# Two expert layers in one kernel: the last experts of a layer taken singly, the closing norm by halves, the first experts found in eights, and ring places freed one at a time

## The chip, the cores and the metric

One core of one Trainium2 chip runs the whole program. The metric is the device time of one execution in microseconds (us).

## The reference

The input is 256 tokens of width 1024, worked on as two tiles of 128 tokens. A first block (pooling, dilated attention, gates) is followed by a second block of two layers. Each of these layers has a mixer (a short convolution in layer 0, windowed attention in layer 1) and then an expert part, which is what the change is about. Cut to it:

```python
def _peer(xn, w_q, subkeys, u_tab, v_tab):            # 8 heads, 128 keys, 16 experts a head
    q = (t @ w_q).reshape(n_tok, PEER_HEADS, 2, SUB_DIM)
    sc = jnp.einsum("thpd,hpnd->thpn", q, subkeys)
    sv, si = lax.top_k(sc, PEER_TOPK)
    cand = sv[:, :, 0, :, None] + sv[:, :, 1, None, :]      # 16 x 16 candidates
    top_v, pos = lax.top_k(cand, PEER_TOPK)
    idx = jnp.take_along_axis(cidx, pos, axis=-1)
    g = jax.nn.softmax(top_v, axis=-1)
    ...
    h = jnp.einsum("cd,ced->ce", xc, jnp.take(u_tab, ic, axis=0))
    a = gc * jax.nn.gelu(h, approximate=False)
    return jnp.einsum("ce,ced->cd", a, jnp.take(v_tab, ic, axis=0))

for i in range(DEPTH_2):                              # 2 layers
    x = x + mixer_i(_rmsnorm_2(x, ...))
    x = x + _peer(_rmsnorm_2(x, ffn_norm_g[i]), ...)
return _rmsnorm_2(x, final_norm_g)
```

Each token picks 128 experts in each layer, each of them a row of 2048 f32 numbers (1024 for the dot, 1024 for the output).

## The kernel before

**Units, pairs and the ring.** In a layer, a unit is one head of one tile: 16 units (`UNITS`), the first eight for tile 0, the others for tile 1. One gather fetches, for each of the 128 tokens, the row of its e-th expert of the unit: 128 x 2048 f32, 1 MB. `ring` has eight places (`RING`) for such gathers. All steps go by pairs of experts (`GROUP` is 2), eight pairs to a unit and 128 pairs to a layer; n counts them.

**The path of a pair.** GpSimd (POOL) issues two gathers (line 534) once `ring_free` says that the pair that had the places is used up. VectorE (DVE) computes a dot for each expert as it lands (`dots`, line 1508) and raises `dots_done` after the second. ScalarE (ACT) then does `mix`: Gelu of both dots (line 666), the product with the gate for each (line 671), and a diagonal matrix 128 x 128 for each, the identity scaled by that coefficient (line 676). TensorE (PE) multiplies each diagonal with the second half of its expert's row, in two halves of 512 columns, into the tile's accumulator in PSUM (`weighted`, line 1117), and raises `ring_free` after the pair. psA is the accumulator of tile 0, psB that of tile 1.

**Around the pairs.** Between the dots, DVE finds the experts of the next unit (`topk_keys`, `topk_grid`, `topk_pairs`, `topk_onehots`, `topk_experts`; the last raises `expert_ready`, for which the gathers of that unit wait) and its gates. For the first unit of a layer all of these steps run ahead of the first dot. In layer 1 they stand ahead of the attention of tile 1 (`attend(1)`). Query products and other matrix products are spread over the slots n of PE's loop by hand-written tables (`PART_SLOTS`, `Q2_AT`).

**The end of a layer.** After the last pair, `tile_out(1)` adds psB to x (line 1516), ACT squares the row and sums it (`norm`, line 548), DVE makes the reciprocal root from a guessed start and three Newton steps in a chain of small instructions, each waiting for the one before (lines 1256 to 1263), and scales the row (line 1265, or 1268 with gains). In layer 1 this is the final norm, and SP then stores the tile (line 485). In layer 0 it is the norm of the attention: PE turns the tile (`turn(3, 1, xn)`), ACT and DVE copy it out (`turned_out`), and PE computes keys (`tile_keys`), scores and values of tile 1 for `attend(0)`. The row's `queries2_out(0, 1, psC)` on DVE copies out the last queries of tile 0. The bias tables of the attention, `bias2[0]` (POOL's queue, line 540) and `bias2[1]` (SP's), and the output weights `wo2` lie where the ring is, so they are loaded only when `ring_free` says that the layer's last pair is used up.

```python
            # PE between the layers
            for j in (2, 3):
                tile_queries(psC[:, 512:1024], 0, 1, j)
            pe.wait_ge(xn_done, step(4, 1))
            turn(3, 1, xn)
            turned_in(3, 1)
            pe.wait_ge(v2_copied, 1)
            tile_keys(1, 0)
            tile_keys(1, 1)
```

## Time and profile before

| | |
|---|---|
| median of three runs | 1900.3 us (1897.44 to 1901.44) |
| the profiled execution | 1901.83 us, with a span of 1899.9 us |
| mean granted TensorE clock | 0.974 of full |
| PE busy | 1645.2 us, 87% |
| DVE, ACT, POOL busy | 55%, 29%, 32% |
| moved by DMA | 642.53 MB, mean 338 GB/s |
| gathers (queue q0) | 540.92 MB, 69.3% of the 16 engines' span |

The profile is of one execution. Its instructions lie within the span; the execution's own time is 1.9 us longer. A clock of 1.00 is the upper level of TensorE's two (2.4 GHz), 0.50 the lower (1.2 GHz); a stretch with a number between holds some of both.

### The profile page before, as it was taken

What the parts mean: (1) busy time and instruction counts of PE and PEld (TensorE: products, weight loads), DVE (VectorE), ACT (ScalarE), POOL (GpSimd) and SP (SyncE); (2) the same over time, 40 slices, a digit from 0 to 9 for tenths busy, and PEclk for the clock granted to TensorE, in tenths of its full rate; (3) what the DMA queues carried; (4) which work ended last, traced back from release to release, by engine and by line L of the source; (5) the groups of instructions that cost most, each with busy time, mean ns of one, the idle gap of its engine ahead of it and who ended that gap; (6) DMA issues with size and microseconds to landing.
All of it is one profiled execution on the core that took longest, in us unless ns stands there. A gap on an engine that the chain in (4) does not pass through costs nothing.

```text
span 1899.9 us, 18599 instructions
## 1 busy us (share of the span) xinstructions
PE 1645.2 (87%) x6184; PEld 958.7 (50%) x6184; DVE 1048.3 (55%) x2676; ACT 554.5 (29%) x1665; POOL 598.6 (32%) x532
## 2 busy tenths in 40 slices
PE   7999999998779988887987779898998988877776
PEld 6888886985335444443542336653544443333222
DVE  2211202224776666576776643666676667676664
ACT  1211000101333433333334323332333333333332
POOL 1000000002444433345444420143444443454442
PEclk9999999999999999999999999999999998899999
DMA  9444333565999999999999987799999999999996
GB/s 227 128 130 159 113 133 130 182 251 211 421 404 398 421 417 417 417 413 390 421 420 413 421 327 248 299 356 413 420 421 421 411 421 399 412 418 416 421 422 266
DMA packets 152926, 642.53 MB, mean 338 GB/s; under 512 B 9972, under 2 KB 50052, under 8 KB 87037
## 3 DMA queue, kind: packets, MB, share of 16 engines
q0 software_dynamic: 74976, 540.92, 69.3%
q1 hardware_dynamic: 77852, 100.42, 15.9%
q8 instruction: 49, 0.80, 0.2%
q14 instruction: 49, 0.39, 0.1%
HBM read 640.19 MB, written 1.11 MB: 338 GB/s over the span
## 4 chain that ended last, share of the span: by engine, by line
PE 33%; DMA 31%; issue 20%; DVE 9%; ACT 4%; POOL 3%; DVEq 0%; POOLq 0%; ACTq 0%
DMA arena<-in_peer_uv,arena 31%; PE ps L1117 17%; DVE arena L1508 5%; PE ps L813 4%; POOL arena L534 3%; PE ps L824 2%; PE ps L995 2%; ACT arena L676 1%; PE ps L1051 1%; ACT arena L671 1%; PE ps L793 1%; ACT arena L666 1%; PE ps L1041 1%; PE ps L1025 1%; PE ps L1082 0%
## 5 line engine op out<-in xcount | busy, mean ns | idle before, releaser
L1117 PE MATMUL ps<-arena 128*128 128x512 f32 x2048 | 979.1, 624 | 217.5 <-ACT arena L676 217.3
L534 POOL DMA_INDIRECT arena<-in_peer_uv,arena x512 | 587.3, 1147 | 1076.9 <-PE ps L1117 580.3
L1508 DVE CUSTOM_DVE_ANT_0 arena<-xn,arena 128x1024 f32<-128x1024 f32 x512 | 622.2, 1225 | 372.3 <-DMA arena<-in_peer_uv,arena 361.1
L1117 PEld LDWEIGHTS ps<-arena 128*128 128x128 f32 x2048 | 385.9, 197 | 755.7 <-issue 401.8
L666 ACT ACTIVATE arena<-arena 128x2 f32<-128x2 f32 x256 | 52.1, 204 | 822.3 <-DVE arena L1508 821.9
L676 ACT ACTIVATE arena<-const,arena 128x128 f32<-128x128 f32 x512 | 177.5, 394 | 8.3
L793 PE MATMUL ps<-hT,wbuf 128*128 128x256 f32 x704 | 153.0, 379 | 1.1 <-DMA wbuf<-in_w_in 1.1
L793 PEld LDWEIGHTS ps<-hT,wbuf 128*128 128x128 f32 x704 | 133.4, 190 | 19.7 <-issue 1.5
L671 ACT ACTIVATE arena<-arena 128x1 f32<-128x1 f32 x512 | 123.2, 288 | 8.4
L995 PEld LDWEIGHTS ps<-hT,wbuf 128*128 128x128 f32 x736 | 88.2, 192 | 18.7 <-issue 17.7
L995 PE MATMUL ps<-hT,wbuf 128*128 128x128 f32 x736 | 88.7, 275 | 0.8 <-ACT hT L555 0.8
L813 PE MATMUL ps<-hT,wbuf 128*128 128x256 f32 x384 | 85.6, 385 | 1.5 <-ACT hT L558 1.5
L813 PEld LDWEIGHTS ps<-hT,wbuf 128*128 128x128 f32 x384 | 73.8, 193 | 12.8 <-ACT hT L558 1.8
L1329 DVE COPY arena<-ps 128x384 f32<-128x384 f32 x16 | 8.6, 555 | 108.4 <-PE ps L850 107.5
L781 PE MATMUL ps<-wbuf,arena 128*128 128x512 f32 x128 | 55.7, 593 | 0.3 <-DVE arena L1400 0.3
L517 POOL DMA_DIRECT2D arena<-in_w_pool x1 | 0.8, 782 | 148.9 <-DVE arena L1336 148.9
L1398 DVE TENSOR_TENSOR arena<-ps,arena 128x1024 f32<-128x1024 f32 x2 | 2.5, 1225 | 78.2 <-PE ps L793 78.2
L824 PE MATMUL ps<-wbuf,arena 128*128 128x256 f32 (+1 forms) x256 | 43.0, 329 | 0.0
L548 ACT ACTIVATE xn<-x 128x1024 f32<-128x1024 f32 x14 | 14.7, 1052 | 95.9 <-DVE x L1292 78.1
L1508 DVE DVE_READ_ACCUMULATOR2_ANT arena<- 128x1 f32 x512 | 42.5, 83 | 0.0
L666 ACT ACT_TABLE_LOAD x32 | 41.1, 1283 | 0.6
L824 PEld LDWEIGHTS ps<-wbuf,arena 128*128 128x128 f32 x256 | 38.9, 191 | 3.6
(158 smaller groups left out, 1147.9 us busy)
## 6 DMA issues: line engine op xcount, KB each, us to landing
wbuf<-in_w_in SPq DMA_DIRECT2D x36, 512.0 KB, 6.6
wbuf<-in_w_in SPq DMA_DIRECT2D x7, 2048.0 KB, 8.9
wbuf<-in_conv_w_in SPq DMA_DIRECT2D x6, 2048.0 KB, 7.9
wbuf<-in_peer_w_q SPq DMA_DIRECT2D x6, 2048.0 KB, 8.6
arena<-in_peer_uv,arena POOLq DMA_INDIRECT x512, 10.8
wbuf<-in_attn_w_qkv SPq DMA_DIRECT2D x3, 2048.0 KB, 28.7
arena<-in_attn_w_o SPq DMA_DIRECT2D x3, 2048.0 KB, 13.0
wbuf<-in_w_out SPq DMA_DIRECT2D x2, 2048.0 KB, 10.4
```

The source lines that it names most:

```text
L534: pool.indirect_dma_start(ring[:, e % RING], None, A["peer_uv"], bass.IndirectOffsetOnAxis(ap=expert[:, unit % 2, e:e + 1], axis=0))\
L666: nc.scalar.activation(act_e[:, b, e0:e0 + GROUP], dot[:, b, e0:e0 + GROUP], ACT.Gelu).then_inc(gelu_done, 1)
L671: last = nc.scalar.activation(coef[:, b, e:e + 1], act_e[:, b, e:e + 1], ACT.Copy, scale=gate[:, b, e:e + 1])
L676: nc.scalar.activation(diag[:, e % RING], ident, ACT.Copy, scale=coef[:, b, e:e + 1]).then_inc(diag_done, 1)
L781: last = mm(ps[t][:, j * 512:(j + 1) * 512], src[:, k, t * P:(t + 1) * P], wbuf[:, b, k], start=(k == 0), stop=(k == KC - 1))
L793: last = mm(dst[:, m * SEQ:(m + 1) * SEQ], wbuf[:, b, k, m * P:(m + 1) * P], src[:, k - k0], start=(k == k0), stop=(k == k1 - 1))
L813: last = mm(dst[:, g * SEQ:(g + 1) * SEQ], wbuf[:, b, k, g * P:(g + 1) * P], hT[:, k], start=(k == 0), stop=(k == KC - 1))
L824: last = mm(psB[:, t * 512 + cols_of.start:t * 512 + cols_of.stop], hT4[:, k, t, first:first + P], wbuf[:, 2, k, cols_of], start=(k == 0), ...
L995: last = mm(products[:, m - first], w[:, k, m * P:(m + 1) * P], hT[:, k, t * P:(t + 1) * P], start=(k == 0), stop=(k == KC - 1))
L1025: last = mm(psA[:, c * P:(c + 1) * P], wbuf[:, b, k, c * P:(c + 1) * P], hT[:, k, t * P:(t + 1) * P], start=(k == 0), stop=(k == KC - 1))
L1117: last = mm(ps[t][:, s * 512:(s + 1) * 512], diag[:, e % RING], ring[:, e % RING, D + s * 512:D + (s + 1) * 512], start=False, stop=False, ...
L1508: last = nc.vector.tensor_tensor_reduce(out=ring[:, e % RING, 0:D], in0=xn[:, v // PEER_HEADS], in1=ring[:, e % RING, 0:D], scale=1.0, sca ...
```

## The change

- **Singles.** The last four experts of a layer (`SINGLES` = 2 pairs) are mixed one by one (`mix_single`). Their gates are put into four diagonals beforehand (`gate_diagonals`, after pair 125 of the layer), so that the coefficient's own instruction falls away: the expert's diagonal is the gate's diagonal scaled by the Gelu. DVE raises `dots_done` for each of these four. `pair_value` counts the semaphore so.
- **Halves.** At the end of a layer, x of tile 1 is added up in two halves of 512 columns. The first waits only for the first half of the last expert's product (`out_half`). ACT squares each half as it comes (`norm_in_halves`), DVE scales each half by itself, and the last store is made in two. In layer 0, PE turns the tile in two halves.
- **Newton.** The chain of every norm is one instruction shorter: scale factors are folded into the first instruction and the constants.
- **First experts in eights.** The first unit of each layer finds its first eight experts wholly, then the other eight; `expert_ready` rises after each. In layer 1 `queries2_out(1, 1, psD)` stands between the two. The maximum for the softmax (`first_largest`) comes after both.
- **Ring places singly.** `ring_free` rises after each expert, and POOL waits for a place before each gather, no longer before each pair of them.
- **Queries.** The second of the four `tile_queries` of chunk 1 leaves the loop (it was in slot 98) and comes behind the layer; the last is divided around `turn(3, 1)`. On DVE, `turned_out(3, 1)` comes ahead of `queries2_out(0, 1)`.
- ACT's preparatory Exp (line 700) moves behind the squares.

```diff
-NEWTON = (-0.7162417485413143, 0.7348672461377994, -0.7937005259840998)
+NEWTON = (3.0, 12.0, 768.0)
...
                 for unit in range(UNITS * layer, UNITS * (layer + 1)):
-                    pool.wait_ge(expert_ready, unit + 1)
+                    pool.wait_ge(expert_ready, unit + layer + (1 if unit == UNITS * layer else 2))
                     for g in range(UNIT_GROUPS):
-                        pool.wait_ge(ring_free, unit * UNIT_GROUPS + g + 1)
+                        if unit == UNITS * layer and g == UNIT_GROUPS // 2:
+                            pool.wait_ge(expert_ready, unit + layer + 2)
                         if unit == UNITS and g == RING_GROUPS - 1:
                             pool.wait_ge(max2_done, 2 * HEADS2)
-                        pool.sem_inc(pool_waited, 1)
                         for e in range(g * GROUP, (g + 1) * GROUP):
+                            pool.wait_ge(ring_free, unit * TOPK + e + 1)
+                            pool.sem_inc(pool_waited, 1)
                             pool.indirect_dma_start(ring[:, e % RING], None, A["peer_uv"],
...
+            def norm_in_halves(layer):
+                act.wait_ge(x_half, layer + 1)
+                nc.scalar.activation(xn[:, 1, 0:512], x[:, 1, 0:512], ACT.Square, accum_out=small[:, 56:57]).then_inc(sumsq_half, 1)
+                act.wait_ge(x_added, (6, 10)[layer])
+                nc.scalar.activation(xn[:, 1, 512:D], x[:, 1, 512:D], ACT.Square, accum_out=sumsq[:, 1:2]).then_inc(sumsq_done, 1)
...
+                def gate_diagonals(unit):
+                    for i in range(SINGLES * GROUP):
+                        e = TOPK - SINGLES * GROUP + i
+                        last = nc.scalar.activation(gate_diag[:, i], ident, ACT.Copy, scale=gate[:, unit % 2, e:e + 1])
+                    last.then_inc(gate_spread, 1)
+                def mix_single(unit, e):
+                    n, b = (unit - base) * UNIT_GROUPS + e // GROUP, unit % 2
+                    act.wait_ge(dots_done, pair_value(layer, n, e % GROUP))
+                    nc.scalar.activation(act_e[:, b, e:e + 1], dot[:, b, e:e + 1], ACT.Gelu).then_inc(gelu_done, 1)
+                    act.wait_ge(gelu_done, pair_value(layer, n, e % GROUP))
+                    act.wait_ge(gate_spread, layer + 1)
+                    act.wait_ge(ring_free, unit * TOPK + e + 1)
+                    nc.scalar.activation(diag[:, e % RING], gate_diag[:, e - (TOPK - SINGLES * GROUP)], ACT.Copy, scale=act_e[:, b, e:e + 1])\
+                        .then_inc(diag_done, 1)
...
-                    last.then_inc(ring_free, 1)
+                            if n - base * UNIT_GROUPS == UNITS * UNIT_GROUPS - 1 and e == TOPK - 1 and s == 0:
+                                last.then_inc(out_half, 1)
+                        last.then_inc(ring_free, 1)
...
-                            if Q2_AT[c] <= n < Q2_AT[c] + (8, 4)[c] and (n - Q2_AT[c]) % 2 == 0:
+                            if Q2_AT[c] <= n < Q2_AT[c] + (8, 2)[c] and (n - Q2_AT[c]) % 2 == 0:
...
-            for j in (2, 3):
+            for j in (1, 2):
                 tile_queries(psC[:, 512:1024], 0, 1, j)
-            pe.wait_ge(xn_done, step(4, 1))
-            turn(3, 1, xn)
+            tile_queries(psC[:, 512:1024], 0, 1, 3, 0, 2)
+            pe.wait_ge(xn_half, 1)
+            turn(3, 1, xn, halves=True)
+            tile_queries(psC[:, 512:1024], 0, 1, 3, 2, KC)
             turned_in(3, 1)
...
-                tile_out(1)
-                norm((4, 6)[layer], 1, (None, 4)[layer], xn)
+                dve.wait_ge(out_half, layer + 1)
+                nc.vector.tensor_tensor(x[:, 1, 0:512], psB[:, 0:512], x[:, 1, 0:512], ALU.add).then_inc(x_half, 1)
+                dve.wait_ge(ring_free, RING + TOPK * (base + UNITS))
+                nc.vector.tensor_tensor(x[:, 1, 512:D], psB[:, 512:D], x[:, 1, 512:D], ALU.add).then_inc(x_added, 1)
+                norm((4, 6)[layer], 1, (None, 4)[layer], xn, halves=layer)
```

`first_experts(r)`, which takes the place of `topk_pairs`, `topk_onehots` and `topk_experts` for the first unit, does for eight experts at a time what these do for sixteen: a match_replace (only for r = 1), a max, a max_index, two integer operations, four products with one-hot rows, two reductions, and the two steps that make the index.

## Rows read from the trace of the kernel before

**Rows 1.** The page's chain that ended last, by engine, then by line.
```profile
PE 33%; DMA 31%; issue 20%; DVE 9%; ACT 4%; POOL 3%; DVEq 0%; POOLq 0%; ACTq 0%
```

**Rows 2.** Windows of each expert stage: engines busy, clock, DMA share, GB/s.
```profile
455.00:1130.00 675.00, 565.22 (x1714) 275.91 (x1713) 451.24 (x1108) 235.32 (x728) 292.80 (x256) 0.96 1.00 411
1300.00:1885.00 585.00, 482.77 (x1357) 224.35 (x1356) 395.79 (x965) 207.60 (x643) 256.02 (x224) 0.97 1.00 414
```

**Rows 3.** Windows of 4 us in which the DMA engines moved less.
```profile
558.00:562.00 4.00, 4.00 (x22) 2.74 (x21) 3.67 (x10) 2.04 (x8) 1.78 (x2) 1.00 0.90 348
858.00:862.00 4.00, 4.00 (x11) 1.85 (x10) 3.11 (x6) 1.68 (x7) 3.39 (x3) 1.00 0.61 207
1242.00:1246.00 4.00, 4.00 (x18) 2.35 (x17) 3.93 (x9) 1.38 (x5) 3.49 (x2) 1.00 0.51 145
...
1746.00:1750.00 4.00, 3.34 (x9) 1.44 (x8) 2.93 (x7) 0.91 (x5) 3.20 (x3) 1.00 0.91 371
```

**Rows 4.** Timeline of the last pair: start, us, engine, line, form [idle before].
```profile
1884.85 1.22 DVE L1508 CUSTOM_DVE_ANT_0 arena<-xn,arena 128x1024 f32<-128x1024 f32 x1 [1.25 <-DMA arena<-in_peer_uv,arena]
...
1886.12 0.20 ACT L666 ACTIVATE arena<-arena 128x2 f32<-128x2 f32 x1 [3.51 <-DVE arena L1508]
1886.35 0.48 ACT L671 ACTIVATE arena<-arena 128x1 f32<-128x1 f32 x2
1886.87 0.69 ACT L676 ACTIVATE arena<-const,arena 128x128 f32<-128x128 f32 x2
...
1887.32 3.70 PE L1117 MATMUL ps<-arena 128*128 128x512 f32 x8 [1.25 <-ACT arena L676]
```

**Rows 5.** Timeline from the last product to the store.
```profile
1891.06 1.22 DVE L1516 TENSOR_TENSOR x<-ps,x 128x1024 f32<-128x1024 f32 x1 [4.98 <-PE ps L1117]
1892.32 1.06 ACT L548 ACTIVATE xn<-x 128x1024 f32<-128x1024 f32 x1 [4.76 <-DVE x L1516]
...
1893.50 0.15 DVE L1256 TENSOR_SCALAR meansq<-sumsq 128x1 f32<-128x1 f32 x1 [1.22 <-ACT xn L548]
...
1895.60 1.28 DVE L1268 SCALAR_TENSOR_TENSOR xn<-x,rinv,gain_row 128x1024 f32<-128x1024 f32 x1
1896.91 0.34 SPq L485 DMA_DIRECT2D out<-xn  x1
```

**Rows 6.** Timeline between the layers: PE, POOL and DVE.
```profile
1130.92 3.70 PE L1117 MATMUL ps<-arena 128*128 128x512 f32 x8 [1.25 <-ACT arena L676]
1134.45 3.73 PE L1041 MATMUL ps<-hT,wbuf 128*128 128x128 f32 x32
1134.92 1.21 POOL L540 DMA_DIRECT2D arena<-bias_rows  x1 [16.84 <-PE ps L1117]
1142.37 6.48 PE L1025 MATMUL ps<-hT,wbuf 128*128 128x128 f32 x32 [1.26 <-ACT hT L558]
1150.48 3.72 PE L1033 MATMUL ps<-wbuf,hT 128*128 128x256 f32 x16
1150.82 0.43 DVE L1592 CUSTOM_DVE_ANT_0 arena<-ps,arena 128x257 f32<-128x257 f32 x1 [8.32 <-DMA arena<-bias_rows]
1154.76 0.66 PE L1071 MATMUL ps<-const,arena 128*128 128x128 f32 x4
```

**Rows 7.** A window between the layers; its last three columns as in Rows 2.
```profile
1142.00:1146.00 4.00, 3.63 (x17) 3.67 (x18) 0.49 (x6) 0.28 (x2) 0.00 (x0) 0.50 0.99 333
```

**Rows 8.** Timeline of the first experts of layer 0 (DVE), then POOL's gathers.
```profile
451.14 0.42 DVE L1467 TENSOR_TENSOR arena<-arena 128x256 f32<-128x256 f32 x1
451.71 0.43 DVE L1444 MAX8 arena<-arena 128x8 f32<-128x256 f32 x1
...
457.65 0.18 DVE L1495 TENSOR_TENSOR arena<-arena 128x16 uint32<-128x16 f32 x1
...
458.80 1.03 POOL L534 DMA_INDIRECT arena<-in_peer_uv,arena  x1 [266.52 <-issue]
...
461.43 0.94 POOL L534 DMA_INDIRECT arena<-in_peer_uv,arena  x1 [0.30 <-issue]
```

**Rows 9.** Window of the first gathers.
```profile
456.00:460.00 4.00, 4.00 (x26) 3.04 (x26) 1.72 (x5) 0.74 (x2) 1.03 (x1) 1.00 1.01 379
```

**Rows 10.** Timeline: DVE's first row of `attend(1)`, behind the first experts of layer 1.
```profile
1209.03 0.43 DVE L1592 CUSTOM_DVE_ANT_0 arena<-ps,arena 128x257 f32<-128x257 f32 x1 [1.27 <-issue]
```

More of the change, by code:

```diff
@@ L108, in done_value, with pair_value @@
     return sum(1 for u in range(use + 1) if (b, u) not in FREED_BY)
+def pair_value(layer, n, i=0):
+    return layer * (UNITS * UNIT_GROUPS + SINGLES) + n + max(0, n - (UNITS * UNIT_GROUPS - SINGLES)) + i + 1
 def step(norm, tile):
@@ L1034, in tile_values, with tile_queries @@
                 last.then_inc(kv2_done, 1)
-            def tile_queries(dst, t, c, j):
+            def tile_queries(dst, t, c, j, first=0, end=KC):
                 b, use = Q_FILLS[c]
                 pe.wait_ge(w_landed[b], landed_value(b, use))
-                for k in range(KC):
+                for k in range(first, end):
                     last = mm(dst[:, j * P:(j + 1) * P], wbuf[:, b, k, j * P:(j + 1) * P], hT[:, k, t * P:(t + 1) * P], start=(k == 0), stop=(k == KC - 1))
-                if j == 3:
+                if j == 3 and end == KC:
                     last.then_inc(q2_done, 1)
@@ L1264, in norm @@
-                if gains is None:
-                    nc.vector.tensor_scalar(dst[:, t], x[:, t], z, None, ALU.mult).then_inc(xn_done, 1)
-                else:
+                    link(nc.vector.scalar_tensor_tensor(out=to, in0=z, scalar=three, in1=y, op0=ALU.add, op1=ALU.mult))
+                if gains is not None:
                     dve.wait_ge(gain_loaded, 16 * gains)
-                    nc.vector.scalar_tensor_tensor(out=dst[:, t], in0=x[:, t], scalar=z, in1=gain_row[:],
-                                                   op0=ALU.mult, op1=ALU.mult).then_inc(xn_done, 1)
+                for part in (slice(0, D),) if halves is None else (slice(0, 512), slice(512, D)):
+                    if gains is None:
+                        last = nc.vector.tensor_scalar(dst[:, t, part], x[:, t, part], z, None, ALU.mult)
+                    else:
+                        last = nc.vector.scalar_tensor_tensor(out=dst[:, t, part], in0=x[:, t, part], scalar=z, in1=gain_row[:, part],
+                                                              op0=ALU.mult, op1=ALU.mult)
+                    if part.stop < D:
+                        last.then_inc(xn_half, 1)
```

118 lines of the change are left out of this document (85 added, 33 removed).

## Prediction

> **What bounds the kernel.** I read the page's chain first: PE and the gathers hold about a third each [rows 1], so no single engine is the bound throughout. The windows by stage come next. In both expert stages the DMA engines are busy for the whole time and move 411 and 414 GB/s [rows 2]. In undisturbed stretches the same column stands at 421, and a gather of 1.05 MB takes 2.49 us. PE is busy for 84% (565.22 of 675) and 83% of these stages, DVE for 67% and 68%. So the gathers set the pace, and an edit inside these stages is worth only what it gives back of the bandwidth that is missing. I then cut 450 to 1900 us into windows of 4 us and looked for those below 421 [rows 3]. From 558 to 1750 us, leaving out the change of layers, 33 windows fall short by more than 0.15 us of transfer each. What they lack, (421 - rate)/421 x 4 us, comes to 9.7 us in layer 0, 8.1 us in the first 60 us of layer 1 and 5.6 us later, 23 us in all. In some the engines are idle (shares of 0.51 and 0.61), in others busy but slow; the reader is to see that only the former are waiting for POOL. Last come the timelines of the places where no gather runs: the two ends of a layer [rows 4 to 6] and its start [rows 8 to 10]. There every microsecond counts.
>
> **The end of the program.** The last dot starts at 1884.85, and ACT starts at 1886.12 [rows 4]. Before, Gelu, two gate products and the first diagonal lead to PE at 1887.32. The gate products (1886.35 to 1886.87) fall away: 0.52 us. PE needs 3.70 us for 8 records of two experts, which are 0.43 each and 0.26 of pipeline. The last expert alone has four: 1.98 us, with its first half after 1.12. So PE runs from 1886.80 to 1888.78, its first half ends at 1887.92, and 2.24 us are won.
>
> The rest by halves [rows 5]. An add of 256 columns takes 0.42 [rows 8] and one of 1024 takes 1.22, so one of 512 takes 0.69. The first half of x is added from 1887.96 to 1888.65, the second from 1888.82 to 1889.51 (1892.28 before). ACT's square with its sum takes 1.18 for 1024 columns up to the next DVE start; I take 0.70 for a half, which makes 1890.25 for the second (1893.50 before). The chain is ten instructions in 2.10 us; one is gone, and the first becomes a dearer form of about 0.07 more: 1.96, to 1892.2. The scaling takes 1.28; two halves of 0.75 that overlap by the pipeline's 0.1 give the second at 1893.6, where it was 1896.9. The store took 3.0 us from its issue to the span's end, and what is left to store is half. I take 2.7 for it: the end is at 1896.3, 3.6 before 1899.9. Bounds: with a store no shorter and each half dearer by 0.1, 2.8; with a store shorter by what half of its 512 KB takes at 421 GB/s, 0.6 us, 3.9. I take 3.5. The four gate diagonals, 4 x 0.35 = 1.4 us of ACT, lie in ACT's idle 3.5 us of each pair. Without that cover they would cost 1.4 once a layer.
>
> The Trainium skill, in "DMA: Bandwidth & Descriptors", section "Anatomy of one DMA — SWDGE (gpsimd) path", says that a transfer has a fixed part of about 2.0 us which its size doesn't shorten. The store here goes by SP's queue; by that rule it would keep 2.4 of its 3.0 us, and the gain at the end would be 3.9 and not 3.5.
>
> **The change of layers.** The same first steps apply: the last products end 2.2 us earlier, at 1132.4 instead of 1134.6 [rows 6]. The rest shortens to 3.3 us by the scaled row. PE fills the wait with two and a quarter `tile_queries` (3.73 + 0.5), then turns the tile, then does the other three quarters, so `tile_keys` starts at about 1139.0 instead of 1142.4. But this isn't what `attend(0)` waits for. DVE's first row starts at 1150.82, having waited for `bias2[0]`, which POOL issued at 1134.92. That load is released by the last expert's `ring_free`, so it moves by 2.2 us and no more; SP's loads of 4 MB beside it move alike, and the stall goes from keys to bias wholly. What is won on top: before, `tile_values(1)` ran from 1150.48 to 1154.2 after the keys, and the first turn of probabilities came behind it at 1154.76. With keys and scores done by 1144.4, these 3.7 us fall into the wait for the bias, and the first turn is limited by DVE and ACT, at about 1151.0. PE's chain from there on has few gaps. The gain is 2.2 if that chain is not shortened, 3.8 if it is in full; I take 3.0.
>
> Under this stands PE's clock. The keys' 32 records took 6.48 us, against 3.73 for the 32 of the queries, at a clock of 0.50 [rows 6, 7], after gaps of 1.8 and 1.3 us ahead of them. In the changed kernel those gaps close, but a new one opens from about 1148 to 1151, with one short product in it. "TensorE: Matmul & The Clock Gate", section "HAM oscillation — how this bites in real kernels", of the Trainium skill says that waits between short bursts of products bring the clock to its lower level and that the next burst then starts slow. By that rule the price is paid at 1151 and not at 1142; by the rows alone it is 2.75 us (6.48 - 3.73), which would leave +0.2 of the 3.0.
>
> **The first experts.** After the grid (started 451.14), DVE worked to 457.83 for all sixteen [rows 8]. Eight of them need a max, an index, and one-hots of 128 elements; with 0.28 for 128 elements against 0.42 for 256, I come to 455.2, so the first gather may go 2.65 us earlier. What would it meet? The DMA engines are already busy at 1.01 in 456 to 460, with 379 GB/s [rows 9], because a 2 MB load of query weights is under way. A busy server that gets the same bytes earlier ends at the same time. I take 0.2; the bounds are 0 and 2.65. In layer 1 the gathers start earlier too, but dots wait for the end of `attend(1)`, and six gathers done early wait in the ring: 0. The second eight cost DVE 4.1 us, to about 1209.2 after its other savings, and DVE's row at 1209.03 had 1.27 us of idle time before it [rows 10]. So `attend(1)`, behind it in DVE's queue, and with it PE and the first dots, start 0.15 later; the softmax waiting on ACT for `first_largest` has the same delay. Without that 1.27 it would be 1.4.
>
> **Ring places singly.** A pair's first place comes free 1.72 us (4 x 0.43) before its second, and up to twice that at the lower clock. The second gather of a pair can start sooner because POOL, at 0.94 + 0.30 = 1.24 us a gather [rows 8], has issued the first already. So both go at least 1.24 us earlier. Where the DMA is saturated this only lengthens its queue: 0. Where all gathers have landed before the next is issued, the idle time shrinks by 1.24 or to zero. The 23 us fall into ten interruptions, and the smaller of loss and 1.24 in each adds up to about 8. Two of the ten are stretches in which PE itself is the bound (5.22 us a pair against 4.97), where the lead is only partly kept, and some windows are slow without being idle. I take 6; below, 0 (all slow, none waiting); above, 12 (places freed at the slow clock).
>
> **Small ones.** The shorter chain gives 0.19 a norm: two at the start of the program, 0.4; one before `turn(4, 0)`, 0.2; those of layer 0's convolution lie behind PE's matrix products, and those inside expert stages behind gathers, 0. The moved table load (1.3 us on ACT) lies in ACT's wait for `turn(3, 1)`. The `tile_queries` taken out of slot 98 gives PE room that it doesn't need.
>
> **The sum.** 3.5 + 3.0 + 0.2 - 0.15 + 6 + 0.4 + 0.2 = 13.15 us. The profiled execution, at 1901.83, is 1.5 above the median of the runs, 1900.3. From the former 1888.7, from the latter 1887.2; I say 1888.0.
>
> **Rivals.** (a) The ring gives nothing, because the missing bandwidth is slow transfer and not late issue; for it speak windows with shares of 0.9 and rates of 348 to 371 [rows 3], against it those with 0.51 and 0.61. Then 7.1 is won: 1893.9. (b) PE's clock falls in the new wait of `attend(0)`, as above: 1890.8. (c) The lead is worth its upper bound at every interruption: 1882. (d) Slower: the gathers' rate falls, since more of them are under way at once. For it speaks that the engines moved only 333 GB/s at a share of 0.99 when four loads ran together [rows 7]; against it, that the rate is 421 with four or five gathers waiting. Its price is 13 us for each 1.0% of 1260 us. It cancels everything at 1.0%, that is at 417 GB/s in the undisturbed stretches, and at 1.5% gives 1907. (e) The change does nothing that shows: the ring gives nothing and the ends give half, 1896.7.
>
> **Chances.** Forecast (gains of 9 to 17) 0.58; (a) 0.15; (b) 0.12; (c) 0.07; (d) 0.03; (e) 0.05. This measurement can tell 0.2%, 3.8 us, from no change. The forecast, (a), (b) and (c) are all faster, 0.92, of which I take off 0.02 for (a)'s edge; (e) and that edge are the same, 0.07; (d) is slower, 0.03. The range of 1881 to 1896 holds the forecast, (a), (b) and most of (c).
>
> **What would show it.** `bias2[0]`'s reader starts 2.2 us nearer to the last dot than the 21 us of before; the span ends within about 12 us of the last dot's start, not 15; windows below 421 lack about 17 us instead of 23 in all; the first gather goes 2.6 us earlier while the tenth does not. The prediction is wrong if undisturbed windows no longer stand at 421, if the number of windows at a clock below 1.00 changes much, or if the idle windows stay as they are.

## The result and the profile after

The changed kernel takes **1887.0 us** (median of six runs, 1885.12 to 1890.58) beside 1900.78 for the kernel before in six runs on the same chip: a ratio of 0.9936, with a 95% interval of 0.9926 to 0.9946. Its profiled execution has a span of 1888.8 us where the span of before was 1899.9: 11.1 us less, while the medians differ by 13.8. The profiled execution of after, at 1890.58, is the slowest of its six.

To divide this, both traces were cut at five marks: the start of the last grid of layer 0's first unit, the last dot of layer 0, DVE's first row of `attend(0)`, PE's first product of `turn(4, 0)`, and DVE's first row of `attend(1)`. Each interval is the difference of two rows' starts.

| us | before | after |
|---|---|---|
| program start to the grid | 451.14 | 449.06 |
| grid to the last dot of layer 0 | 677.31 | 674.54 |
| last dot to the first row of `attend(0)` | 22.37 | 22.01 |
| that row to `turn(4, 0)` | 37.91 | 37.80 |
| `turn(4, 0)` to the first row of `attend(1)` | 20.30 | 20.32 |
| that row to the first dot of layer 1 | 17.46 | 18.77 |
| first to last dot of layer 1 | 658.36 | 654.91 |
| last dot to the end of the span | 15.05 | 11.39 |

The stage windows of the profile after (us, busy time and records of PE, PE's loads, DVE, ACT and POOL, clock, DMA share, GB/s) answer to [rows 2]:

```profile
454.00:1127.00 673.00, 563.43 (x1697) 274.32 (x1696) 450.52 (x1112) 237.26 (x733) 313.00 (x256) 0.97 1.00 412
1297.00:1878.00 581.00, 473.89 (x1355) 221.11 (x1354) 393.57 (x959) 204.75 (x639) 275.83 (x222) 0.99 1.00 414
```

The mean rates are nearly what they were, 412 and 414 GB/s beside 411 and 414. The page's row of GB/s in 40 slices still has 421 wherever nothing disturbs:

```profile
GB/s 241 127 122 165 105 134 131 182 250 212 421 417 408 421 417 417 417 417 418 401 421 411 422 333 247 284 378 409 420 421 421 421 419 408 411 421 413 400 422 302
```

The timeline of the end (start, duration, engine, line, form, idle before) answers to [rows 4, 5]:

```profile
1877.41 1.23 DVE L1601 CUSTOM_DVE_ANT_0 arena<-xn,arena 128x1024 f32<-128x1024 f32 x1 [1.25 <-DMA arena<-in_peer_uv,arena]
...
1878.91 0.40 ACT L719 ACTIVATE arena<-arena 128x128 f32<-128x128 f32 x1
...
1879.36 1.99 PE L1168 MATMUL ps<-arena 128*128 128x512 f32 x4 [0.49 <-ACT arena L719]
...
1881.38 0.69 DVE L1675 TENSOR_TENSOR x<-ps,x 128x512 f32<-128x512 f32 x1 [0.17 <-PE ps L1168]
...
1882.94 0.16 DVE L1317 SCALAR_TENSOR_TENSOR meansq<-sumsq,small 128x1 f32<-128x1 f32 x1 [0.78 <-ACT xn L574]
...
1884.86 1.42 DVE L1331 SCALAR_TENSOR_TENSOR xn<-x,rinv,gain_row 128x512 f32<-128x512 f32 x2
...
1886.30 0.33 SPq L502 DMA_DIRECT2D out<-xn  x1
```

The reader is to see that PE starts 1.95 us after the last dot (2.47 before), works 1.99 instead of 3.70, and that DVE adds the second half 0.17 us after it has ended the first.

The timeline between the layers answers to [rows 6]:

```profile
1127.84 1.21 POOL L559 DMA_DIRECT2D arena<-bias_rows  x1 [15.85 <-PE ps L1168]
...
1133.96 3.81 PE L1076 MATMUL ps<-hT,wbuf 128*128 128x128 f32 x32
...
1139.40 3.72 PE L1084 MATMUL ps<-wbuf,hT 128*128 128x256 f32 x16
1145.61 0.43 DVE L1693 CUSTOM_DVE_ANT_0 arena<-ps,arena 128x257 f32<-128x257 f32 x1 [10.61 <-DMA arena<-bias_rows]
...
1146.45 1.22 PE L1113 MATMUL ps<-arena 64*128 64x256 f32 x4 [3.33 <-DVE small L1693]
...
1148.09 1.11 PE L1122 MATMUL ps<-const,arena 128*128 128x128 f32 x4 [0.41 <-DVE arena L1703]
```

and two windows of the same stretch to [rows 7]:

```profile
1142.00:1146.00 4.00, 1.12 (x6) 0.64 (x4) 0.39 (x3) 0.00 (x0) 0.00 (x0) 0.98 1.04 380
...
1148.00:1152.00 4.00, 3.92 (x18) 2.61 (x20) 2.90 (x15) 2.56 (x10) 0.00 (x0) 0.50 1.09 349
```

The keys now take 3.81 us instead of 6.48, at the upper clock. After them come a short product and the values (3.72 us), then PE is idle for 3.33 us, and what follows runs at 0.50: its turns of four records take 1.11 us where they took 0.66. POOL issued the bias load 4.24 us after the last dot's start instead of 6.47, but the row that reads it starts 17.8 us after the issue, against 15.9 before. So in this execution nothing of the 2.2 us shows.

The first experts of layer 0 answer to [rows 8, 9]; first POOL's and DVE's timeline, then the windows:

```profile
454.04 1.03 POOL L553 DMA_INDIRECT arena<-in_peer_uv,arena  x1 [263.83 <-issue]
...
462.56 1.23 DVE L1601 CUSTOM_DVE_ANT_0 arena<-xn,arena 128x1024 f32<-128x1024 f32 x1 [2.36 <-DMA arena<-in_peer_uv,arena]
```

```profile
452.00:456.00 4.00, 4.00 (x33) 3.59 (x32) 3.39 (x16) 0.38 (x1) 1.65 (x2) 1.00 0.72 229
456.00:460.00 4.00, 4.00 (x31) 3.46 (x30) 1.29 (x8) 2.07 (x4) 3.08 (x4) 1.00 1.07 420
```

The first gather goes 4.98 us after the grid instead of 7.66. The window at 456 shows 420 GB/s where [rows 9] had 379, but it lies 2.1 us later from the grid. At equal distances the rates are 389 and 379 (from 4.9 to 8.9 us after the grid), then 415 and 384 (from 6.9 to 10.9).

### The profile page after: what moved, and what is told of

Its sections match the earlier page's. It is cut to its first block, busy times and chain, and to the rows that moved or that the text cites. A ratio compares the mean times of both kernels' runs of the same rounds, so it can differ in the third digit from the quotient of the medians.

```text
span 1888.8 us, 18883 instructions
## 1 busy us (share of the span) xinstructions
PE 1632.7 (86%) x6184; PEld 954.6 (51%) x6184; DVE 1048.6 (56%) x2690; ACT 556.7 (29%) x1673; POOL 638.7 (34%) x532
## 3 DMA queue, kind: packets, MB, share of 16 engines
q1 hardware_dynamic: 77996, 100.42, 16.1%
HBM read 640.19 MB, written 1.11 MB: 340 GB/s over the span
## 4 chain that ended last, share of the span: by engine, by line
PE 39%; DMA 37%; DVE 9%; issue 8%; ACT 3%; POOL 3%; DVEq 0%; POOLq 0%; SPq 0%; ACTq 0%
DMA arena<-in_peer_uv,arena 35%; PE ps L1168 11%; PE ps L844 9%; DVE arena L1601 5%; PE ps L864 4%; POOL arena L553 3%; PE ps L832 3%; PE ps L875 2%; PE ps L1046 2%; PE ps L821 2%; PE ps L1102 1%; ACT arena L702 1%; DMA arena<-bias_rows 1%; ACT arena L697 1%; DMA wbuf<-in_w_in 1%
## 5 line engine op out<-in xcount | busy, mean ns | idle before, releaser
L1168 PE MATMUL ps<-arena 128*128 128x512 f32 x2048 | 966.7, 618 | 220.5 <-ACT arena L702 219.1
L553 POOL DMA_INDIRECT arena<-in_peer_uv,arena x512 | 627.5, 1225 | 1031.1 <-PE ps L1168 549.3
L1601 DVE CUSTOM_DVE_ANT_0 arena<-xn,arena 128x1024 f32<-128x1024 f32 x512 | 621.8, 1225 | 364.4 <-DMA arena<-in_peer_uv,arena 352.5
L844 PEld LDWEIGHTS ps<-hT,wbuf 128*128 128x128 f32 x704 | 133.8, 191 | 19.2 <-issue 1.5
L1046 PEld LDWEIGHTS ps<-hT,wbuf 128*128 128x128 f32 x736 | 88.3, 192 | 19.2 <-issue 18.2
## 6 DMA issues: line engine op xcount, KB each, us to landing
wbuf<-in_peer_w_q SPq DMA_DIRECT2D x6, 2048.0 KB, 10.5
```

The source lines that it names most:

```text
L553: pool.indirect_dma_start(ring[:, e % RING], None, A["peer_uv"], bass.IndirectOffsetOnAxis(ap=expert[:, unit % 2, e:e + 1], axis=0))\
L844: last = mm(dst[:, m * SEQ:(m + 1) * SEQ], wbuf[:, b, k, m * P:(m + 1) * P], src[:, k - k0], start=(k == k0), stop=(k == k1 - 1))
L1046: last = mm(products[:, m - first], w[:, k, m * P:(m + 1) * P], hT[:, k, t * P:(t + 1) * P], start=(k == 0), stop=(k == KC - 1))
L1168: last = mm(ps[t][:, s * 512:(s + 1) * 512], diag[:, e % RING], ring[:, e % RING, D + s * 512:D + (s + 1) * 512], start=False, stop=False, ...
L1601: last = nc.vector.tensor_tensor_reduce(out=ring[:, e % RING, 0:D], in0=xn[:, v // PEER_HEADS], in1=ring[:, e % RING, 0:D], scale=1.0, sca ...
```

## The experiments

Three groups of runs, each on one chip with its own runs of the kernel before. The whole change was measured in groups 2 and 3 only, so kernels of group 1 are compared with it by their ratios. Medians and ratios to before:

| kernel | us | ratio, 95% interval |
|---|---|---|
| group 1, before 1904.24 | | |
| `ring_pairs` | 1899.02 | 0.9964, 0.9952 to 0.9976 |
| `no_eights` | 1889.42 | 0.9920, 0.9905 to 0.9935 |
| `no_singles` | 1895.81 | 0.9948, 0.9934 to 0.9962 |
| `bias_early` | 1887.92 | 0.9916, 0.9899 to 0.9932 |
| group 2, before 1906.56 | | |
| `before_again` (one run) | 1904.34 | |
| `after_again` | 1890.44 | 0.9917, 0.9904 to 0.9931 |
| `hold_gathers` | 1897.25 | 0.9953, 0.9938 to 0.9968 |
| `warm_wait` | 1889.56 | 0.9914, 0.9900 to 0.9927 |
| group 3, before 1904.47 | | |
| `ring_only` | 1898.51 | 0.9969, 0.9959 to 0.9980 |
| `ends_only` | 1898.33 | 0.9972, 0.9961 to 0.9982 |
| `after_third` | 1892.44 | 0.9932, 0.9919 to 0.9945 |
| `bias_early_again` | 1889.75 | 0.9922, 0.9910 to 0.9933 |

The intervals of their profiled executions, at the same marks (row 0 is the first row of `attend(0)`, row 1 that of `attend(1)`; "lacking" is the sum of (421 - rate)/421 x 4 us over the windows of both expert stages, as in the prediction; cutting the windows elsewhere moves an entry by up to 2 us). Each row is one profile:

| us | stage L0 | dot to row 0 | row 0 to turn | row 1 to first dot | row 1 to last dot | tail | lacking |
|---|---|---|---|---|---|---|---|
| before | 677.3 | 22.4 | 37.9 | 17.5 | 675.8 | 15.05 | 23.9 |
| `before_again` | 681.5 | 22.1 | 36.4 | 21.4 | 675.6 | 15.05 | 26.0 |
| `ring_only` | 675.8 | 22.7 | 36.5 | 19.2 | 671.7 | 15.03 | 14.2 |
| `ends_only` | 680.2 | 19.5 | 36.2 | 19.1 | 673.3 | 11.32 | 23.7 |
| `ring_pairs` | 678.2 | 20.5 | 38.5 | 22.0 | 678.6 | 11.38 | 25.5 |
| `no_eights` | 675.7 | 20.0 | 36.2 | 20.8 | 673.8 | 11.39 | 14.8 |
| `no_singles` | 674.1 | 22.0 | 36.2 | 22.4 | 677.4 | 13.63 | 15.6 |
| after | 674.5 | 22.0 | 37.8 | 18.8 | 673.7 | 11.39 | 17.7 |
| `after_again` | 673.8 | 19.7 | 37.3 | 21.8 | 675.1 | 11.33 | 14.7 |
| `after_third` | 674.4 | 19.6 | 36.2 | 22.3 | 676.5 | 11.37 | 15.5 |
| `bias_early` | 673.2 | 15.6 | 38.3 | 21.9 | 676.7 | 11.37 | 14.1 |
| `bias_early_again` | 673.5 | 15.6 | 38.2 | 21.3 | 675.7 | 11.41 | 14.5 |
| `hold_gathers` | 674.1 | 19.7 | 36.2 | 20.6 | 682.4 | 11.39 | 10.5 |
| `warm_wait` | 673.3 | 19.6 | 37.7 | 21.9 | 676.3 | 11.38 | |

**`ring_pairs`** is the changed kernel with POOL waiting for both places of a pair again.

```diff
-                            pool.wait_ge(ring_free, unit * TOPK + e + 1)
+                            if e % GROUP == 0:
+                                pool.wait_ge(ring_free, unit * TOPK + e + GROUP)
```

> The changed kernel, but GpSimd again waits for both places of a pair before it issues the pair's first gather; all else is kept. If ring places freed singly are worth the 6 us of the prediction, this runs 6 us above the changed kernel's 1887.0, at 1893, and the idle windows of 4 us come back (shares of 0.5 to 0.8, a total loss near 23 us between the start of the gathers and 1750 us). If the missing bandwidth is slow transfer and not late issue, it runs at 1887, within 1 us. The traces of before and after already put the whole gain of the two expert stages at about 6 us (2.8 and 3.5), so I expect 1890 to 1893.

Its 1899.02 us lie above that range, but the kernel before is slower on this chip too (1904.24 beside 1900.78). By ratio it loses 5.3 to 9.0 us against the three measurements of the whole change (0.9964 beside 0.9917 to 0.9936), and 25.5 us are lacking again.

**`ring_only`** is the opposite: the kernel before, with `ring_free` raised after each expert and awaited for each gather, and nothing else of the change.

```diff
-                        pool.wait_ge(ring_free, unit * UNIT_GROUPS + g + 1)
...
                         for e in range(g * GROUP, (g + 1) * GROUP):
+                            pool.wait_ge(ring_free, unit * TOPK + e + 1)
...
-                    last.then_inc(ring_free, 1)
+                        last.then_inc(ring_free, 1)
```

> The kernel before with one part of the change: its ring places come free one expert at a time, and GpSimd waits for each expert's own place. No new first experts, no gates in diagonals, no halves, no moved bias load. Undoing this part alone in the changed kernel gave 1899.02 us beside 1889 to 1890 for the whole, which says that it is worth some 5 to 9 us there. If it is worth the same by itself (my theory: the gathers start sooner after each free place wherever the ring holds them back, and need nothing else of the change), this kernel lies about 5 us below the one before, a ratio of 0.9965 to 0.9975, and the tail stays at 15.05 us. Rival: the places singly only help when the first experts of a stage come in eights, because the lead gained there is then kept: the ratio is 0.9985 or above.

It wins 6.0 us by itself (1904.47 to 1898.51), as expected; the rival's 0.9985 lies outside the interval. Its tail is that of before. The column "lacking" divides the table in two: 23.7 to 26.0 us in the four profiles with pairs, 14.1 to 17.7 in those with single places (`hold_gathers` apart). The windows of one interruption, where a new unit's keys meet the loop, in `ends_only` (pairs) and then in `ring_only` (singly):

```profile
860.00:864.00 4.00, 4.00 (x11) 1.84 (x10) 3.25 (x7) 1.38 (x5) 1.78 (x2) 0.98 0.38 119
```

```profile
856.00:860.00 4.00, 4.00 (x10) 1.71 (x10) 3.63 (x9) 1.03 (x5) 2.33 (x3) 0.99 0.91 348
860.00:864.00 4.00, 4.00 (x10) 1.71 (x9) 3.18 (x9) 1.73 (x7) 3.39 (x3) 1.00 1.03 360
```

With pairs the DMA engines stood idle for more than half of 4 us (share 0.38), and POOL, busy for 1.78, waited. With single places POOL is busy for 2.33 and 3.39 us, and what is left is mostly slow transfer.

**`ends_only`** has what remains: the changed kernel with the places in pairs and the first unit's experts found sixteen at once (the edits of `ring_pairs` and `no_eights`).

> The changed kernel without its two gather parts: the ring places come free in pairs again, and the first experts of a layer are found sixteen at once. What is left is the single experts at the end of each layer, the rows by halves, the earlier bias load and the order of queries. If the parts add up (whole 13 to 16 us, ring 5 to 6, eights 2), this kernel lies 6.5 to 8.5 us below the one before, ratio 0.9955 to 0.9966; 3.6 us of that are the tail, which shall be 11.4 us instead of 15.05. Rival: the end alone (3.6 us) and nothing at the change of layers, because PE's clock falls there in the new wait: ratio 0.9981.

It wins 6.1 us, a little less than the 6.5 to 8.5 expected. With the 6.0 of `ring_only` that makes 12.1, and the whole change wins 12.0 on the same chip (1892.44). Nothing is left for the eights, as far as these numbers reach: each of the three has an interval of about 2 us to either side.

**`no_eights`** is the changed kernel with `topk_pairs`, `topk_onehots` and `topk_experts(0)` for the first unit.

```diff
-                    pool.wait_ge(expert_ready, unit + layer + (1 if unit == UNITS * layer else 2))
+                    pool.wait_ge(expert_ready, unit + 1)
...
-                first_experts(0)
+                topk_pairs()
+                topk_onehots()
+                topk_experts(0)
...
-                first_experts(1)
-                first_largest()
```

> The changed kernel with the first sixteen experts of a layer found in one go, as before; all else is kept. If the DMA engines are a busy server at that time, the first gathers are issued 2.65 us later and nothing else moves: 1887, within 0.5. In the rival the early start carries through the whole of layer 0's stage, because it sets when the eight first places are refilled: 1889 to 1890. In layer 1 neither expects anything but 0.1 us at the start of the attention of tile 1.

Its ratio, 0.9920, is no worse than the three of the whole change (0.9936, 0.9917, 0.9932). Yet the table shows two differences that cancel, each read from two profiles without eights. Layer 0's stage takes 675.7 and 675.8 us in the two kernels with single places and no eights, and 673.2 to 674.5 in the eight with both: 1.9 less in the mean. And from row 1 to the last dot the same two take 673.8 and 671.7, the others, without `hold_gathers`, 673.7 to 677.4, in the mean 675.9: 3.1 more in layer 1. With pairs the latter is the same (678.6 in `ring_pairs`, 673.3 to 675.8 in the other three).

Layer 0's difference isn't the eights' alone. ACT's copy of the query products, behind which the scores of the next unit and the first mixing come, starts late in most profiles, though PE's products for it are done or stand still short of their end. Four rows of it, from `before`, `before_again`, `no_eights` and `after_third`:

```profile
466.80 0.60 ACT L641 ACTIVATE arena<-ps 128x512 f32<-128x512 f32 x1 [5.05 <-PE ps L995]
```

```profile
470.75 0.60 ACT L641 ACTIVATE arena<-ps 128x512 f32<-128x512 f32 x1 [8.65 <-remote]
```

```profile
470.25 0.60 ACT L665 ACTIVATE arena<-ps 128x512 f32<-128x512 f32 x1 [8.81 <-remote]
```

```profile
469.56 0.60 ACT L667 ACTIVATE arena<-ps 128x512 f32<-128x512 f32 x1 [6.34 <-PE ps L1046]
```

Counted from the grid, it starts at 15.7 us in the first profiles of before and of after, at 19.1 to 19.4 in the four others without eights, and at 16.9 to 17.3 in the eight others with them. The later it starts, the later the first places come free: the ninth gather goes at 29.3 and 29.6 us in `ring_only` and `no_eights`, and at 24.9 to 27.4 in the kernels with eights and single places. `before` and `before_again`, one kernel, differ by 4.2 us in layer 0's stage, with this row at 15.7 and 19.3. Whether finding experts in eights shortens this standstill, or something else in these kernels does, no run shows.

**`no_singles`** sets `SINGLES` to 0; the halves stay.

```diff
-    SINGLES = 2
+    SINGLES = 0
```

> The changed kernel with no experts taken singly: the last pairs go by pairs to the end, without gate diagonals; the halves stay. At the end of the program the last products start 0.5 us later and hold two experts, so all of the tail is 2.2 us later; at the change of layers the bias load is issued 2.2 us later. If both are on the path: 4.4 us, 1891.4. If the change of layers is bound by something that doesn't move with it (TensorE's clock, or how the loads share the engines): 2.2 us, 1889.2.

By ratio it loses 2.3 to 5.9 us against the whole change, and both of the places expected to pay do: row 0 comes 2.3 and 2.4 us later than in `after_again` and `after_third`. The tail is 13.63, 2.24 more than after, which is the predicted size of this step to the hundredth; its timeline has the two gate products again:

```profile
1882.28 0.48 ACT L697 ACTIVATE arena<-arena 128x1 f32<-128x1 f32 x2
1882.79 0.69 ACT L702 ACTIVATE arena<-const,arena 128x128 f32<-128x128 f32 x2
1883.24 3.70 PE L1168 MATMUL ps<-arena 128*128 128x512 f32 x8 [1.26 <-ACT arena L702]
```

**`bias_early` and `bias_early_again`** are one kernel: POOL's wait ahead of layer 1's bias load asks for two places fewer.

```diff
-            pool.wait_ge(ring_free, RING + UNITS * TOPK)
+            pool.wait_ge(ring_free, RING + UNITS * TOPK - 2)
```

> The changed kernel, with one number altered: the load of bias2[0], whose area in the ring is places 0 to 2, is issued when two experts are still to be used, not when all are. It goes out about 4 us earlier, into the time in which the DMA engines stand still after the last gather. If attend(0) waits for this load alone, its first row comes 4 us or more earlier, PE no longer waits 3.3 us before it and stays at its upper clock, and the time falls by 5 to 6 us, to 1881.5. The rival is that the load shares the engines with the last gathers and holds the last dots up: then at most 1 us is won, or nothing.

> The changed kernel with layer 1's bias load issued one unit earlier still: GpSimd's wait ahead of it asks for two ring places fewer than all. In its one profile so far the first row of layer 1 came 15.6 us after layer 0's last dot product instead of 19.7 to 22.0, and its time was 1.5 us below that of the kernel without eights, which is 1888 to 1889 where the whole change is measured. If the landing of this bias sets the start of layer 1 (theory), it lies 2 to 3 us below the whole change on this chip. Rival: its landing is hidden by the wait for the keys' products and by the stalls that follow in the first third of layer 1's attend, and the two are within 1 us.

Row 0 comes 15.6 us after the last dot in both, 4.0 sooner than in `after_again` and `after_third`, and now waits for PE:

```profile
1139.73 0.43 DVE L1693 CUSTOM_DVE_ANT_0 arena<-ps,arena 128x257 f32<-128x257 f32 x1 [4.21 <-PE ps L1113]
```

But 2.0 of the 4.0 go again before the turn (38.2 instead of 36.2), since `tile_values` (3.72 us) then stands in front of `attend(0)`'s first products. Beside `after_third` on the same chip it wins 2.7 us (1889.75), where 5 to 6 had been expected at first; the intervals of the two ratios overlap, and on the other chips the ratios of `bias_early` and `after_again` are alike (0.9916 and 0.9917). So the landing of this bias did set row 0, and after this edit PE does; what that is worth in all isn't settled.

**`after_again`, `after_third` and `before_again`** are the two kernels unchanged, for the spread of each interval.

> The kernel before, once more, for a second profile. Its time should be that of before, and the stretches of the trace should repeat: 677 us from the first unit's grid of candidates to layer 0's last dot, 60.3 from there to the turn of layer 1, 17.5 from the first row of attend(1) to layer 1's first dot, 658 to the last dot, 15.05 to the end. Where TensorE's clock differs from the first profile, that stretch differs: I expect the first 48 products in 10.6 or in 12.3 us, and that this has nothing to do with the change.

> The changed kernel, once more and on the same chip as the other three of this call: ratio 0.9936 again. In its profile, PE waits about 3.3 us for the bias in attend(0). If that wait brings the clock down, attend(0) shows products at 0.50 again and 59.8 us from the last dot to the turn; if the fall in the first profile was chance, it is 56.5.

> The changed kernel once more, on the same chip as the other three, as the one that they are compared with: ratio to the kernel before 0.9917 to 0.9936.

The stretches of before did not repeat: layer 0's stage took 677.3 and then 681.5 us, row 0 to the turn 37.9 and then 36.4, row 1 to the first dot 17.5 (the shortest of all) and then 21.4. In the changed kernel row 0 came late in the first profile only (22.0, then 19.7 and 19.6). Of PE at the change of layers they show (`after_again`, then `after_third`):

```profile
1144.85 0.70 PE L1113 MATMUL ps<-arena 64*128 64x256 f32 x4 [1.02 <-DVE small L1693]
1146.49 0.66 PE L1122 MATMUL ps<-const,arena 128*128 128x128 f32 x4 [0.94 <-DVE arena L1703]
1147.08 1.22 PE L1113 MATMUL ps<-arena 64*128 64x256 f32 x4
1148.23 1.12 PE L1122 MATMUL ps<-const,arena 128*128 128x128 f32 x4
```

```profile
1147.40 0.70 PE L1113 MATMUL ps<-arena 64*128 64x256 f32 x4 [0.92 <-DVE small L1693]
1149.04 0.66 PE L1122 MATMUL ps<-const,arena 128*128 128x128 f32 x4 [0.93 <-DVE arena L1703]
1149.62 0.70 PE L1113 MATMUL ps<-arena 64*128 64x256 f32 x4
```

The same products after nearly the same gaps: in the one execution the clock falls to its lower level for the third burst, in the other it doesn't. Where it fell, row 0 to the turn took 37.3 and 37.8, where not, 36.2. Eight profiles of the changed kernel and its variants have this wait with nothing put into it. PE's idle time just before the first of these products was 3.33 us (`after`), 1.83 (`ring_pairs`) and 1.02 (`after_again`) where the clock fell, and 0.86 to 1.33 in the five where it stayed up, so among gaps of about 1 us the length doesn't decide.

**`warm_wait`** makes the products of `tile_values(1)` twice, so that PE works on in the wait; the second time overwrites the first.

> The changed kernel, with the 16 products of tile_values(1) made twice, into the same place, the first time without use: 3.7 us more of PE's work where PE waits 3.3 us for the bias. If the wait is what brings the clock down, the clock stays at 1.00, the first turns of attend(0) take 0.66 and not 1.11 us, and the stretch from the last dot to the turn of layer 1 is 56.5 to 57 us instead of 59.8, so 2 to 3 us are won. If the clock falls for another reason, nothing is won and 0.4 us lost.

The clock stayed up (the first turn took 0.66 us), but row 0 to the turn still took 37.7: the second 3.7 us of products end after row 0 and stand in the way. The 2 to 3 us expected did not come: it ties with `after_again`. Nor does its one profile show that the products kept the clock up, since five profiles without them kept it too.

**`hold_gathers`** lets none of layer 1's gathers start before `attend(1)` has read the place of the seventh; six of them started early before.

```diff
-                        if unit == UNITS and g == RING_GROUPS - 1:
+                        if unit == UNITS and g == 0:
```

> The changed kernel, but in layer 1 no gather goes out before the last row maximum of attend(1); in the changed kernel six of them do. Four of the profiles so far show waits of 1.2 to 2.0 us of DVE in the first third of attend(1) for which no engine's work accounts, while these gathers run. If the gathers cause them, they are absent here, and attend(1) takes 17.2 to 17.5 us from its first row to its last copy instead of 18.8 to 22.4; the first dot then comes late by the time of a first gather, about 1 to 2 us after attend(1). On the whole 2 us slower to 1 us faster than the changed kernel. If code or chance causes them, they are still there, and it is 2 to 5 us slower.

It asked whether those gathers cause the waits in `attend(1)`. Row 1 to the first dot takes 20.6 us, within the range of the others, but the waits moved. Before POOL's first gather, which goes 12.9 us after row 1, there is none. Behind it come two, ahead of the rows at 17.2 and 20.1 us, where the same rows wait only 1.17 and 0.85 us in `before`:

```profile
1215.89 0.96 POOL L553 DMA_INDIRECT arena<-in_peer_uv,arena  x1 [83.68 <-issue]
...
1220.17 0.29 DVE L1709 COPY hT<-ps 128x128 f32<-128x128 f32 x1 [2.74 <-remote]
...
1223.05 0.29 DVE L1709 COPY hT<-ps 128x128 f32<-128x128 f32 x1 [2.59 <-remote]
```

So this run speaks for a link with the gathers and not against one; it is one profile, and `before` and `after` have the same early gathers without such waits. The kernel costs 6.8 us (1897.25 against 1890.44), more than the 2 to 5 expected at worst. Two windows of 60 us each from the first dots on, of `hold_gathers` and then of `after_again`, say where:

```profile
1226.00:1286.00 60.00, 54.73 (x176) 28.02 (x175) 39.07 (x106) 19.18 (x61) 23.06 (x20) 0.98 1.02 417
```

```profile
1224.00:1284.00 60.00, 55.99 (x184) 28.78 (x183) 44.12 (x117) 20.61 (x66) 24.01 (x21) 1.00 0.98 378
```

Six gathers are 14.9 us of transfer. Done early they save 6.8: in the next 60 us the engines of `after_again`, whose ring is full at the start, move 378 GB/s instead of 417, which gives 5.6 us back. The remaining 2.5 us were not traced.

## Why the prediction was right

**The end: 3.5 predicted, 3.66 measured** in the span, 3.64 to 3.73 in the repetitions. By its steps, counted from the last dot's start: PE 1.95 predicted and 1.95 measured, second add 3.97 and 3.97, second sum of squares 5.40 and 5.53, start of the scaling 7.35 and 7.45, second store 8.75 and 8.89, end 11.45 and 11.39. What the squares and the scaling took more (0.14) the store gave back: 2.50 us from its issue to the span's end and not 2.7. The Trainium skill's fixed part of a transfer ("DMA: Bandwidth & Descriptors", "Anatomy of one DMA — SWDGE (gpsimd) path") had given 2.4 as an estimate, nearer than my own.

**The change of layers: 3.0 predicted, 0.5 in the first pair of profiles, 3.0 where the clock stays up** (from the last dot to the turn 58.5 and 59.2 us in `before_again` and `ring_only`, 55.9 in the mean of `ends_only`, `no_eights`, `after_third` and `hold_gathers`). The whole came out, its two parts didn't quite. Row 0 moved by more than the 2.2 of the load: 22.1 to 22.7 us from the last dot without the change, 19.5 to 20.0 in six of the eight profiles whose kernel has singles and the bias load as changed; the other two are 20.5 and 22.0. The load is issued 2.23 us nearer to the last dot in all of them, and its own time from issue to reader varies from 15.3 to 17.8. (The prediction's "21 us of before" counts from the dot's end; from its start it is 22.4.) Of what `tile_values` was to bring, 0.8 in the sum and at most 1.6, 0.2 came (36.4 and 36.5 to 36.2). The step read that from the first profile of before, in which the clock of the keys had fallen and pushed the values behind row 0. In `before_again` they ended with the wait, in `ring_only`, with keys of 5.44 us, a microsecond behind it, and row 0 to the turn was as short. Rival (b) is real: the clock did fall in the new wait, in two of the three profiles of the changed kernel, at 1.1 and 1.6 us each, and in `ring_pairs`, at 2.3. That is less than its 2.75. The Trainium skill's rule on waits between short bursts ("TensorE: Matmul & The Clock Gate", "HAM oscillation — how this bites in real kernels") agrees with `after`, where the clock was down right behind the wait of 3.33 us; for waits of about 1 us the traces show it as a risk and not as a certainty: `after_third` has the same gaps as `after_again` and keeps its clock.

**Ring places singly: 6 predicted, 6.0 measured** by `ring_only`. The mechanism held too: idle windows shrank and slow ones stayed. But "23 us lacking, about 17 with the change" was right only in the first profile (23.9 and 17.7). In the means, 24.8 and 15.1 are lacking, 9.7 less, of which 6 are won. So a third of that isn't on the path; I haven't shown where it goes. Rivals (a), 0, and (c), 12, are both out.

**First experts in eights: 0.2 predicted, 0 within the intervals, and not by the mechanism that I gave.** "A busy server that gets the same bytes earlier ends at the same time" is not quite so. Up to 28 us after the grid the engines have moved 9.69 to 9.80 MB in the nine profiles with eights and 9.30 to 9.60 in the five without, which is 0.2 to 1.2 us of transfer at 421 GB/s. One of the signs named beforehand came out otherwise, too: the tenth gather was not to go earlier, but it goes at 26.8 us after the grid instead of 28.1 in the first pair of profiles (the places taken singly may have done that). The tenth dot starts 36.8 us after the grid in `after` and `after_third`, 38.6 and 39.4 in `no_eights` and `ring_only`, but 37.2 in `before`, which has neither eights nor the standstill of ACT's row. So where that standstill is absent 0.4 us are left, and how much of layer 0's 1.9 the eights have won is open. In layer 1, which I had at 0, about 3 us are lost, 1.5 of them before the first dot (20.0 in the mean of two, 21.5 in that of seven). The 0.15 expected at the first row of `attend(1)` is 0.02, so the loss isn't in that queue. Part of it lies in standstills inside `attend(1)`: with eights most profiles have two, of 1.2 and 1.3 us, and a mean clock of 0.72 to 0.83 in its first 8 us, against one of 1.9 and a clock of 1.00 without. The cause stays open. That the net is what the prediction said is luck.

**The small ones.** The shorter chain brought 0.36 of the 0.4 at the start: PE's second stretch of products began at 14.32 instead of 14.68. The other 1.7 us by which the first profile of after was early at the grid are no part of the change: its first 48 products took 10.60 us against 12.32. Of all fourteen profiles only `warm_wait` has 10.60 too; in the twelve others they took 12.0 to 13.6, and the grid started at 450.6 to 452.7 instead of 449.1. So of the 11.1 us between the first two spans the change made 9.4.

**The other rivals.** (d) is out: undisturbed slices still stand at 421 GB/s. (e) is out with `ring_only` and the tail.

**The sum**, then: 3.7 at the end, 2.4 for the rest of `ends_only`, 6.0 for the ring, 0 for the eights: 12.1, beside 12.0, 13.8 and 16.1 us between medians on the three chips, and 13.15 predicted. The forecast hit by terms that were right singly at the end and at the ring, each with a run that isolates it. The change of layers was right in size, but 0.8 of its 3.0 was argued from one execution's clock and hardly came, and the load's part was larger than its 2.2. The eights' 0.2 was right by luck.

## What stays open

In `attend(1)`, DVE, ACT and PE stand idle together for 1.2 to 2.1 us in every profile but the first two and `hold_gathers`, where more waits come later, and no row accounts for it. The timeline of `ring_only` has it:

```profile
1213.19 0.70 PE L1062 MATMUL ps<-arena 64*128 64x256 f32 x4
1214.71 0.60 ACT L723 ACTIVATE arena<-ps 128x512 f32<-128x512 f32 x1 [1.94 <-remote]
1215.21 0.50 ACT L728 ACTIVATE arena<-arena,small 128x257 f32<-128x257 f32 x1
1215.46 0.63 PE L1071 MATMUL ps<-const,arena 128*128 128x128 f32 x4 [1.56 <-issue]
1215.50 0.29 DVE L1608 COPY hT<-ps 128x128 f32<-128x128 f32 x1 [1.88 <-remote]
```

It is in kernels with and without the change, and it hides up to 4 us of one profile against another; with eights it mostly comes twice (1.2 and 1.3 us) instead of once (1.9), which is part of layer 1's loss. ACT's late row in layer 0, behind the first gathers, is marked "remote" too where it is longest. In `hold_gathers` the standstills came after the gathers had begun and not before, so they may need busy DMA engines. The loading of instructions, for which the profile has two small DMA queues (49 and 50 packets, 1.2 MB), could do it; no run tested that.

## What to carry to other kernels

Where a ring of buffers feeds a saturated queue, free and await its places one by one: here, with eight places, it won 6.0 us of 1904 for some ten changed lines. At the end of a stage, make the last piece of work small for every engine in turn and do the closing norm by halves, which could be costed here from the rows to within 0.2 us. A DMA share near 1.0 doesn't say that the engines move all they can (0.98 stood beside 378 GB/s in `after_again`, 1.02 beside 417 in `hold_gathers`): look at the GB/s beside it before calling earlier work worthless. Before a stretch of some microseconds is argued from one profile, take a second one: clock and standstills moved the same stretch by 1.5 to 4 us between two profiles of one kernel. And where a run was to remove a wait, look for where the wait went, not only at the length of the stretch.

## What the runs showed of the hardware

- TensorE's granted clock fell after two gaps of 1.02 and 0.94 us in `after_again` and after 1.83 and 0.93 in `ring_pairs`; it stayed up after 0.92 and 0.93 in `after_third` and after 1.33 and 0.93 in `no_eights`.
- The first 48 products of the program took 10.60 us in two profiles and 12.0 to 13.6 in twelve, whatever the kernel, which moves all that follows by 1.4 us and more.
- Engines stood idle together with no row to account for it, for up to 3.7 us in layer 0 (ACT's row at 19.4 instead of 15.7 us after the grid) and up to 2.1 us in `attend(1)`; in `hold_gathers` the latter came only once gathers were under way.
- The same bias load took 15.4 us from issue to reader in `after_again` and 17.8 in the first profile of after, beside the same other loads.
- With single waits a gather's issue on POOL took 1225 ns in the mean instead of 1147, over all 512, and this cost nothing that shows:

```profile
L553 POOL DMA_INDIRECT arena<-in_peer_uv,arena x512 | 627.5, 1225 | 1031.1 <-PE ps L1168 549.3
```
